# S5 lag matrices formed from the turned sources in one stage, M put together by copies within SBUF, and S5 stages and selection rounds at earlier units of the attention loop

## The reference, cut to what matters

```python
# S5 mixer: 32 groups of 16 channels, 64 complex states each, 512 steps
bu = einsum('blgc,gpc->blgp', u, bb)                   # complex, bb = coef * b
x  = associative_scan(x[l] = lb * x[l-1] + bu[l])      # lb = exp(a * dt)
y  = real(einsum('blgp,gcp->blgc', x, c)) + d_skip * u
y  = gelu(y);  y_ssm = y * sigmoid(y @ w_glu + b_glu)

# sparse attention: 8 heads of 64; an indexer picks 128 keys for each query
s_idx  = sum_h relu(qi[h] @ ki.T) * wi[h]              # causal
sel    = top_k(s_idx, 128)
y_attn = softmax(q @ k[sel].T * scale) @ v[sel]
```

## Time and profile before

| | us |
|---|---|
| median of 3 runs | 750.1 (749.08 to 751.55) |
| the profiled execution | 751.51 |
| its span, first to last instruction | 749.7 |
| PE busy | 703.4 (94%) |
| DVE busy | 478.8 (64%) |
| ACT busy | 310.5 (41%) |
| POOL busy | 258.4 (34%) |

### The profile page before, as it was taken

How to read it: one execution, slowest core, us unless ns; L and a number is a source line. 1 busy time by engine, 2 the same in 40 slices (tenths; PEclk the granted TensorE clock), 3 DMA queues, 4 the chain that set the end, 5 groups by cost and what they waited for, 6 DMA issues and landing times.

```text
span 749.7 us, 9853 instructions
## 1 busy us (share of the span) xinstructions
PE 703.4 (94%) x3566; PEld 555.2 (74%) x3566; DVE 478.8 (64%) x818; ACT 310.5 (41%) x487; POOL 258.4 (34%) x211
## 2 busy tenths in 40 slices
PE   0899999999878999999999999999999999999997
PEld 0687777777555656778798888888878887888886
DVE  2868987976999789788757867655654555000005
ACT  4435346745612564723475344344334344122120
POOL 2001899419902400000003443443342442443440
PEclk9899999999987989999899999999999999999999
DMA  9942131260065665826733223323323313313302
GB/s 335 379 127 85 57 112 57 85 196 1 8 71 51 185 237 190 296 76 225 259 106 113 84 84 112 105 63 112 100 68 113 97 71 113 103 66 112 113 1 112
DMA packets 63081, 91.47 MB, mean 122 GB/s; under 512 B 12010, under 2 KB 41474, under 8 KB 62979
## 3 DMA queue, kind: packets, MB, share of 16 engines
q1 hardware_dynamic: 59520, 89.44, 37.8%
q10 hardware_dynamic: 3523, 1.54, 0.7%
HBM read 86.28 MB, written 4.69 MB: 121 GB/s over the span
## 4 chain that ended last, share of the span: by engine, by line
PE 76%; DVE 15%; ACT 3%; issue 2%; DMA 2%; SPq 0%; ACTq 0%; DVEq 0%
PE bank L1615 22%; PE bank L1617 22%; PE bank L1616 22%; PE bank L1620 3%; DVE arena L1318 2%; PE bank L1965 1%; PE bank L1850 1%; DVE stat L1315 1%; DVE w_lo L1167 1%; DVE arena L1157 1%; DVE arena L1181 1%; PE bank L1830 1%; PE bank L1960 1%; DMA stat<-in_k_norm 1%; DMA xh<-in_x 1%
## 5 line engine op out<-in xcount | busy, mean ns | idle before, releaser
L503 POOL TENSOR_TENSOR w_lo<-w_raw,w_hi 128x2048 fp32r<-128x2048 f32 x32 | 147.7, 4616 | 349.1 <-ACT w_hi L1048 280.2
L1615 PE MATMUL bank<-act_hi,w_hi 128*128 128x512 f32 (+1 forms) x384 | 145.3, 378 | 0.1
L1617 PE MATMUL bank<-act_hi,w_lo 128*128 128x512 f32 (+1 forms) x384 | 144.3, 376 | 0.0
L1616 PE MATMUL bank<-act_lo,w_hi 128*128 128x512 f32 (+1 forms) x384 | 144.3, 376 | 0.0
L1615 PE MATMUL bank<-w_hi,act_hi 128*128 128x512 f32 x240 | 101.4, 423 | 1.4 <-DVE act_lo L1207 1.4
L1617 PE MATMUL bank<-w_hi,act_lo 128*128 128x512 f32 x240 | 97.4, 406 | 0.0
L1616 PE MATMUL bank<-w_lo,act_hi 128*128 128x512 f32 x240 | 97.4, 406 | 0.0
L700 ACT ACTIVATE w_hi<-w_raw 128x2048 fp32r<-128x2048 f32 x26 | 49.8, 1914 | 93.9 <-PE bank L1617 90.8
L1615 PEld LDWEIGHTS bank<-act_hi,w_hi 128*128 128x128 f32 x384 | 72.3, 188 | 14.6 <-DVE conv L1571 0.3
L1616 PEld LDWEIGHTS bank<-act_lo,w_hi 128*128 128x128 f32 x384 | 72.4, 188 | 14.3 <-issue 0.2
L1617 PEld LDWEIGHTS bank<-act_hi,w_lo 128*128 128x128 f32 x384 | 72.3, 188 | 14.1
(11 more groups left out here) (314 smaller groups left out, 1143.1 us busy)
## 6 DMA issues: line engine op xcount, KB each, us to landing
w_raw<-in_w_up SPq DMA_DIRECT2D x44, 512.0 KB, 4.7
arena<-in_w_ada SPq DMA_DIRECT2D x18, 1024.0 KB, 8.5
w_raw<-in_w_down SPq DMA_DIRECT2D x22, 512.0 KB, 3.9
w_raw<-in_w_in SPq DMA_DIRECT2D x10, 1024.0 KB, 5.1
xh<-in_x SPq DMA_DIRECT2D x8, 512.0 KB, 7.1
w_raw<-in_w_out SPq DMA_DIRECT2D x4, 1024.0 KB, 10.2
arena<-in_w_ada SPq DMA_DIRECT2D x2, 2048.0 KB, 10.9
arena<-lag_dram SPq DMA_DIRECT2D x16, 128.0 KB, 5.9
```

The source lines that it names most:

```text
L503: nc.gpsimd.tensor_tensor(w_lo[:, slot, 0:width], w_raw[:, slot, 0:width], w_hi[:, slot, 0:width].bitcast(F32), ALU.subtract).then_inc(S[" ...
L1615: T.matmul(dst, lhs_hi, rhs_hi, start=start, stop=False)
L1616: T.matmul(dst, lhs_hi, rhs_lo, start=False, stop=False)
L1617: return T.matmul(dst, lhs_lo, rhs_hi, start=False, stop=stop)
```

## The change

The lag matrices are formed in one stage for both halves, at unit 6. The stationary operand is `s5_vt` (the sources as they were before their transposition, 64 rows by 128 columns: 8 powers times 16 channels), the moving operand is `s5_c`, 16 columns. D is added by a matmul with rows of the identity, so `bb_diag`, `add_d` and the lag-0 part of `lag_w` go, and with them `lag_dram`. The result stands on 128 partitions (8 lags times 16 channels), and M is made by 8 copies for each half within SBUF, each shifted down by 16 partitions; POOL clears what no copy writes, after the stage, since M lies where `s5_vt` was. `u` of half 1 gets memory of its own. `y` now also waits for `lag_w` itself. Stages move: lags 7 and 10 to 6, u 6 and 12 to 7 and 8, states 11 and 13 to 9 and 11; y stays at 14 and 15. Three selection rounds run before the loop, and the others are spread differently. ACT's casts move from units 3 and 5 to 9 and 13.

```diff
-         6: ("u", 0, 0), 7: ("lags", 0, 0), 10: ("lags", 1, 0), 11: ("states", 0, 0), 12: ("u", 1, 0), 13: ("states", 1, 0),
+         6: ("lags", 0, 0), 7: ("u", 0, 0), 8: ("u", 1, 0), 9: ("states", 0, 0), 11: ("states", 1, 0),
          14: ("y", 0, 0), 15: ("y", 1, 0), 18: ("g", 0, 0), 20: ("g", 1, 0),
-ROUNDS = {**{i: 2 for i in range(8)}, **{i: 4 for i in range(8, 12)}, 16: 3, 17: 3, 18: 2, 19: 1, 20: 2, 21: 2, 22: 2, 23: 1}
+AHEAD = (1, 1, 1)
+ROUNDS = {**{i: (1, 1) for i in (0, 1, 2, 4, 5)}, 3: (1, 1, 2, 2, 2), 6: (1, 2), 7: (2, 2),
+          8: (2, 2, 2), 9: (2, 2), 10: (2, 2, 2), 11: (2, 2),
+          **{i: (3, 3) for i in range(13, 18)}, **{i: (3,) for i in range(18, 24)}}
...
-        s5_m = [cut(a, NG, P) for a in (26024, 28072)]
-        s5_u = [v.rearrange("p (g n) -> p g n", g=NG) for v in (s5_mem[:, 4096:5120], up32[:].rearrange("p a n -> p (a n)"))]
+        s5_m = [cut(a, CHUNK, NG, CH) for a in (26024, 28072)]
+        s5_u = [v.rearrange("p (g n) -> p g n", g=NG) for v in (s5_mem[:, 4096:5120], cut(23976, 1024))]
-        lags = [cut(a, GH, CHUNK, CH)[0:2 * CH] for a in (26024, 28072)]
+        lags = cut(22440, 2, GH, 2, CH)
...
@@ sync @@
-            sp.wait_ge(S["zeros_stored"], 32)
+            sp.wait_ge(S["lags_ready"], 2)
+            sp.wait_ge(S["m_zero"], 2)
             for half in range(2):
-                sp.wait_ge(S["lag_d_added"], 2 * half + 2)
-                gs = slice(NG * half, NG * (half + 1))
-                for q in range(2):
-                    sp.dma_start(lag_dram[:, gs].rearrange("c (g q) l h -> c q g l h", q=2)[:, q, :, CHUNK - 1:, :],
-                                 lags[half][CH * q:CH * q + CH]).then_inc(S["lags_stored"], 16)
-                sp.wait_ge(S["lags_stored"], 32 * (half + 1))
-                for j in range(CHUNK):
-                    load(s5_m[half][CH * j:CH * (j + 1)].rearrange("p g (l h) -> p g l h", l=CHUNK),
-                         lag_dram[:, gs, CHUNK - 1 - j:2 * CHUNK - 1 - j, :], "m_loaded")
+                for i in range(CHUNK):
+                    n = CH * (i + 1)
+                    load(s5_m[half][0:n, i], lags[P - n:P, half].rearrange("p g q h -> p (g q) h"), f"m_loaded{half}")
...
@@ gpsimd @@
-            nc.gpsimd.memset(s5_mem[:, 0:2048], 0.0).then_inc(S["zero_ready"], 1)
-            nc.gpsimd.memset(bb_diag, 0.0).then_inc(S["bb_zero"], 1)
...
-                G.tensor_copy(w[:, 0, :, 0, :], s5_c[:, 0, gs])
-                G.tensor_copy(w[:, 1, :, 0, :], s5_c[:, 1, gs])
...
-                for q in range(2):
-                    hp = slice(64 * q, 64 * q + 64)
-                    link(G.tensor_copy(bb_diag[hp, :, :, CH * q:CH * q + CH], s5_bb[hp]))
...
             weigh_lags(0)
+            pool.wait_ge(S["lag_mm"], 1)
+            for half in range(2):
+                G.memset(s5_m[half][:, 0:CHUNK - 1].rearrange("p i g h -> p (i g h)"), 0.0).then_inc(S["m_zero"], 1)
             weigh_lags(1)
...
@@ scalar @@
-            for i in range(2):
-                act.dma_start(lag_dram[:, NG * i:NG * (i + 1), 0:CHUNK - 1, :],
-                              s5_mem[0:CH, 0:NG * (CHUNK - 1) * CH].rearrange("p (g l h) -> p g l h", g=NG, l=CHUNK - 1)
-                              ).then_inc(S["zeros_stored"], 16)
...
                     elif stage == "lags":
-                        act.wait_ge(S["lag_mm"], 2 * half + i + 1)
-                        nc.scalar.activation(lags[half][:, 4 * i:4 * i + 4],
-                                             src[0:2 * CH, :].rearrange("p (g l h) -> p g l h", g=4, l=CHUNK),
+                        act.wait_ge(S["lag_mm"], 1)
+                        nc.scalar.activation(lags[:, :, :, i, :], src[:, 0:256].rearrange("p (b g h) -> p b g h", b=2, g=GH),
                                              ACT.Copy).then_inc(S["lags_ready"], 1)
...
-                if i == 3:
+                if i == 9:
                     hi(U_GLU)
-                if i == 5:
+                if i == 13:
                     hi(U_OUT)
...
@@ vector @@
+            top_k([(t,) for t in AHEAD], ())
...
-                        if stage == "lags" and back == 1:
-                            add_d(half)
...
@@ tensor @@
                 elif stage == "u":
                     pe.wait_ge(S["u_grouped"], 2)
-                    pe.wait_ge(S["v_ready"], 8)
-                    if half:
-                        pe.wait_ge(S["state_read"], 1)
+                    pe.wait_ge(*((S["lags_ready"], 2), (S["u_t_read"], 2))[half])
...
                 elif stage == "lags":
+                    pe.wait_ge(S["bb_ready"], 1)
+                    pe.wait_ge(S["v_ready"], 8)
+                    rows = slice(P - 2 * CH, P)
+                    for q in range(2):
+                        T.matmul(bank[6 + q][:, 0:256].rearrange("p (b g h) -> p b g h", b=2, g=GH), ident[rows, :],
+                                 d_eye[:, :, :, q, :], start=True, stop=False)
+                    for g in range(GP):
+                        for r in range(2):
+                            for q in range(2):
+                                hp = slice(64 * q, 64 * q + 64)
+                                ins = T.matmul(bank[6 + q][:, CH * g:CH * g + CH],
+                                               s5_vt[g // GH][hp, r, g % GH].rearrange("p j h -> p (j h)"),
+                                               s5_c[hp, r, g, :], start=False, stop=(g == GP - 1 and r == 1))
+                    ins.then_inc(S["lag_mm"], 1)
...
                 else:
-                    pe.wait_ge(S["lags_ready"], 2 * half + 2)
-                    pe.wait_ge(S["m_loaded"], 16 * CHUNK * (half + 1))
+                    pe.wait_ge(S["lag_w_ready"], half + 1)
+                    pe.wait_ge(S[f"m_loaded{half}"], 16 * CHUNK)
...
-                            T.matmul(o[NCH * q:NCH * (q + 1)], s5_u[half][:, 2 * g + q, :], s5_m[half][:, 2 * g + q, :],
-                                     start=True, stop=False)
+                            T.matmul(o[NCH * q:NCH * (q + 1)].rearrange("c (i h) -> c i h", i=CHUNK),
+                                     s5_u[half][:, 2 * g + q, :], s5_m[half][:, :, 2 * g + q, :], start=True, stop=False)
```

More of the change, by code:

```diff
@@ L175, in layer @@
         ki_w = cut(19616, TT, TAIL)
-        d_eye = cut(25000, GP, CH)[0:2 * CH]
+        d_eye = cut(25000, 2, GH, 2, CH)[P - 2 * CH:P]
         b_glu_row = cut(25512, 512)[0:1]
@@ L192, in layer @@
         prob, prob_t = cut(14336, 2, 512), cut(15360, 2, 512)
-        lag_w = [cut(16384, 2, GH, CHUNK + 1, CH), cut(12032, 2, GH, CHUNK + 1, CH)]
+        lag_w = [cut(a, 2, GH, CHUNK, CH) for a in (16384, 12032)]
         turn = cut(8192, 2, GP, NCH)
@@ L576, in s5_rest @@
                 cf_r, cf_i, ur, ui, r8, w1, w2, w3, w4 = (s5_p[:, i] for i in (12, 13, 17, 18, 19, 20, 21, 22, 23))
-                mag, sin_t, cos_t, mask = s5_p[:, 1], s5_p[:, 8], s5_p[:, 9], s5_p[0:2 * CH, 2]
+                mag, sin_t, cos_t = s5_p[:, 1], s5_p[:, 8], s5_p[:, 9]
                 def square(o_r, o_i, a_r, a_i):
@@ L651, in _ @@
                 turn_step(n)
-            s5_diagonals()
+            skip_diagonals()
             future(1)
@@ L747, in _ @@
                     load(b_glu_row, ssm_b_glu, "b_rows_loaded")
-                    for q in range(2):
-                        load(d_eye[CH * q:CH * q + CH],
-                             ssm_d[0].rearrange("(g q h) -> q g h", q=2, h=CH)[q].partition_broadcast(CH), "d_loaded")
+                    load(d_eye.rearrange("p b g q h -> p (b g q h)"), ssm_d[0].partition_broadcast(2 * CH), "d_loaded")
                 if k % 4 == 0:
@@ L909, in s5 @@
                         act.wait_ge(S["u_t"], 2 * half + i + 1)
-                        if half and i == 0:
-                            act.wait_ge(S["lag_w_ready"], 2)
                         nc.scalar.activation(s5_u[half][:, 8 * i:8 * i + 8], src[:].rearrange("p (g n) -> p g n", g=8),
@@ L1208, in split @@
                        ready)
-            dve.wait_ge(S["zeros_stored"], 32)
             lr, li, ldt = (vec_cols[:, a:a + GP] for a in (C_ARE, C_AIM, C_LDT))
@@ L1385, in heads_out @@
                                        rinv[:, w].unsqueeze(2).broadcast_to([P, HEADS, HD]), ALU.mult), "y_attn_ready")
-            def add_d(half):
-                for i in range(2):
-                    dve.wait_ge(S["lags_ready"], 2 * half + i + 1)
-                    g = 4 * i
-                    signal(V.tensor_tensor(lags[half][:, g:g + 4, 0, :], lags[half][:, g:g + 4, 0, :],
-                                           d_eye[:, GH * half + g:GH * half + g + 4, :], ALU.add), "lag_d_added")
             def scan(half, part):
@@ L1466, in _ @@
                         stage, half, part = S5_AT.get(j - back, ("none", 0, 0))
-                        if stage == "lags" and back == 1:
-                            add_d(half)
-                        elif stage == "states" and back == 1:
+                        if stage == "states" and back == 1:
```

(27 more changed lines are left out.)

28 lines of the change are left out of this document (11 added, 17 removed).

## The result

The changed kernel takes **761.5 us** (median of 4, 761.04 to 762.59) where the kernel before, run beside it, takes 749.6 (748.09 to 751.55): ratio 1.0207, 95% interval 1.0158 to 1.0255. Ratios are estimated from the fast runs of both kernels, so they need not be the quotient of the two medians shown. The forecast was 758, in a range of 747 to 766. The sign came, and the time lies inside the range, but above the forecast's own 756 to 760: the loss of 11.9 us falls in the band of rival 3 (+10 to +18), which had a chance of 0.12. Nor did it come the way I had worked out: the first matmul of `y` half 0, Y0, is 14.5 us late where I had 7.8, and 4.9 of it came back later, where I had nothing coming back. Profiled: span 759.3 (us 761.51), granted clock 0.966; before 749.7, 0.970.

A forecast was written before the change was run, and what follows sets the result against it. DVE was taken to pace the loop up to the first y matmul and PE after it. That matmul comes 7.8 us later and nothing comes back: 750.1 + 7.8 = 758, range 747 to 766.

The forecast's parts named there:

- rival 3: Lag stage: loads queue or PE runs at 1.2 GHz, stage 14.6 to 17 us, total 764 to 767; chance 0.12.
- What bounds the loop: Loop of 32 attention units: DVE paces the part up to the first y matmul, PE the part after it.
- Up to the lag stage: Units 4 to 9: unit 8's logits at 194.1, DVE ready at 201.2, lag stage begun at 192.2.
- AHEAD: Before the loop: three selection rounds, 2.95 us, move into DVE's gap before the first logits, free.
- The lag stage: PE at unit 6: 128 records at 60 ns plus D, 8.6 us, bounds 5.1 and 14.6 at full clock.
- The lock: scan(0): DVE operations with two SBUF inputs take turns with POOL's weigh_lags, costing 3.6 us, bounds 0 and 8.
- Units 12 and 13: DVE: logits 0.8, all of scan(1) 10.6 and two rounds at 512 keys 3.04, together 14.4 us.
- the signs that I had named: Trace checks, among them PE idle over 20 us between 205 and 243; wrong if lag stage outside 5 to 15.
- After Y0: Rest of the loop behind the first y matmul: order unchanged, PE without idle time, so nothing of the 7.8 us comes back.
- rival 2: After the first y matmul DVE paces, so 9.1 us of removed rounds come back, total 747; chance 0.18.
- SP's copies: SP queue: 16 copies within SBUF, 0.47 us each to issue, issued by 211.6, hidden by 26 us.
- M read with a step of 256: y matmuls: 16 pieces of 16 columns per matmul, cost taken as 0, between 0 and 2 us.

The follow-up runs named there:

- e1: Changed kernel with the imaginary half of the lag matmuls left out, 64 records instead of 128: 754.2 us, ratio 1.0136.
- e6: Changed kernel with the lag stage cut in two halves of 64 records, scans later, weigh_lags(1) ahead, unit 13's rounds given to 14 and 15: 755.6 us, ratio 1.0138.
- e9: Changed kernel with 64 moving columns instead of 16 per lag record, written to columns nobody reads, lag products left out: 758.07 us in a single profiled run.
- e12: e11 with lag records of 64 and 48 moving columns instead of 16 and the skip term as wide, output still correct: 750.2 us, ratio 1.0036.
- e2: Changed kernel with five 128x512 identity matmuls put between the narrow ones of the lag stage: 769.8 us, ratio 1.0305.
- e3: Changed kernel with the states of half 1 back at unit 13, so scan(1) runs behind unit 14's logits: 755.1 us, ratio 1.011.
- e4: Changed kernel with weigh_lags(1) on POOL before its wait for the lag stage: 758.4 us, ratio 1.0169.
- e7: Changed kernel with both scans back at their old places (states at 11 and 13), single lag stage kept: 753.9 us, ratio 1.0122.
- e11: e6 with e8's order of rounds, none between unit 12's logits and scan(1): 753.5 us, ratio 1.0112.
- e10: The kernel before, unedited, profiled once more on e8's chip: 749.45 us.
- e5: Kernel before with only the change's earlier selection (AHEAD) and new distribution of rounds: 747.1 us, ratio 1.0032.
- e8: e5 with the four rounds of units 13 and 14 moved to 15 to 17, so none stand ahead of scan(1): 746.1 us, ratio 1.0041.

## Why the prediction came near, and where it was wrong

**What bounds the loop.** Right: the loss is decided at Y0, DVE paces up to it, PE behind it.

**Up to the lag stage.** Right within 0.8 us, which is the later start of the loop (169.52 against 168.75). AHEAD and unit 3's rounds were free; unit 8's logits 194.68 (forecast 194.1), DVE ready at 201.7 (201.2), the stage begun at 192.87 (192.2).

**The lag stage: the step that failed.** I had 8.6 us and measured 13.63, and the path from its end to logits 10, at the lower level too, 6.4 for 4.2. With the 0.7 of the later start, logits 10 came at 212.9 instead of 205.0: +7.9. The 13.63 lies inside the 5 to 15 us outside which I had called myself wrong: those bounds were drawn at full clock and could not see this. The price of a record was right, 56 to 59 ns against 60, in e1, e6, e9 and e12; what was mis-sized is the level at which it is paid. Rival 3 had the lower level (stage 14.6 to 17), with a chance of 0.12, and I took it from the old stage, where PE had been idle ahead. Here PE was not. In the seven kernels with 16-column records in full number (the changed one, e2, e3, e4, e6, e7, e11), the clock fell within 4.1 us of the first record; in the two with 48 or 64 columns, one profile each, it did not fall in the stage; e1's 64 records were followed by a fall as e6's were. That it depends on what the records stream is shown by the pair e9 and after, and again by e12 and e11; why it does so was not measured. The five wide matmuls of e2 did not help; whether more of them would is open.
The Trainium skill, "TensorE: Matmul & The Clock Gate", section "HAM oscillation — how this bites in real kernels", puts the fall down to stretches in which TensorE sits idle. In this case's trace PE is busy 13.63 of 13.63 us and the clock falls at 195.5; the measurement decides: a busy share of 100% in the profile is no guarantee. By the same page's section "LDWEIGHTS (loading the stationary operand)", which I had weighed, the 128 loads would take 13.7 us at full clock, an estimate from its figure. e9 measured 7.36 us for 128 records, each load 188 ns long and the next one begun after 57: loads overlap more than that rule has it. That they do so because they alternate between the row halves is my reading; no run leaves the alternation out. That the page's figure lies at the measured 13.6 is coincidence.

**The lock.** Too dear: 1.65 us instead of 3.6, inside its bounds, because POOL had shifted with the stage and only one operation met scan(0). In e9, where the stage was on time, it cost 3.8.

**Units 12 and 13** took 14.5 us (forecast 14.4); unit 14's logits to Y0 2.5 (1.9), at the lower level. The sum: +7.9 - 1.9 + 0.1 + 0.6 = 6.7, from 243.5 to 250.2. Of the signs that I had named, one more failed by a little: from the stage's end to Y0 PE idled 19.1 us, not over 20.

**After Y0.** "Nothing comes back" was wrong by 4.9 us. 3.7 of them lie in the loop, beyond the 3 that I had named as a refutation, but not for rival 2's reason (DVE pacing there). The stretches from Y0 to unit 31's logits, of before, of before again (e10) and of after:

```profile
235.74:306.19 70.45, 67.32 (x438) 43.87 (x438) 61.73 (x119) 36.82 (x81) 9.03 (x2) 0.90 0.53 182
```
```profile
235.17:302.97 67.80, 64.40 (x431) 41.86 (x432) 61.56 (x117) 36.02 (x79) 9.02 (x2) 0.95 0.54 185
```
```profile
250.19:316.91 66.72, 62.28 (x439) 41.08 (x438) 49.36 (x96) 36.76 (x81) 3.65 (x1) 0.98 0.55 194
```

DVE has 12 us less to do in the last than in the first two (49.36), and that bought nothing visible: the same program needs 2.65 us less when its clock is 0.95 and not 0.90, and the changed one continues that line at 0.98. The other runs agree: e2, with DVE as little busy as in the changed kernel (49.4 us) but the clock at 0.93, takes 68.2 us, and e3, with DVE at 57.5 and the clock at 0.95, 67.2. Of the 4.9 us, 3.7 came back here and the rest behind the loop, where before has one low stretch of 6.8 us and after one of 3.4. So PE paces, as I had it, and the level decides how fast. That the median came within 3.5 us of 758 is partly luck: this gift, which I had not foreseen, and the cheaper lock stood against the dearer stage.

**SP's copies** took 0.63 us each to issue, not 0.47; issued by 219.9 for a Y0 at 250, hidden as forecast. M read with a step of 256 showed no cost. A piece is 16 columns and a matmul reads 8 of them, not the 16 of the prediction; the four records of a group with M take 0.44 us at full clock before (242.41) and in e3 alike, and 0.69 at the lower level before and after (Y0's own row):

```profile
242.41 0.44 PE L1960 MATMUL bank<-arena,s_mem 128*64 128x128 f32 x4
```
```profile
246.61 0.44 PE L1930 MATMUL bank<-arena,s_mem 128*64 128x128 f32 x4
```

**What stays open.** Timed, e5, e8 and e12 stand at 1.003 to 1.004. From unit 4's to unit 31's logits e8 takes 118.9 us and e12 117.3, but e10, the kernel before, 117.4: at its better clock it has nothing left to win here. Timed runs of before lie between 739 us at 0.99 and 757 at 0.97, those of e12 between 744 at 0.98 and 761 at 0.96; where the low stretches lie in the timed runs no trace shows.

## What to carry to other kernels

Price a stage of many small matmuls at both levels of TensorE's clock, and look at the granted clock in the trace rather than at its busy share: here a record's price doubled in the middle of the stage (56 to 107 ns) with the engine 100% busy. Where records are paid by their loads, streaming more columns into unused PSUM may cost nothing: here 128 records took 7.4 us with 64 columns each, and the clock stayed full in the stage, though not behind it. Before moving work of the pacing engine ahead of a consumer, list every gate of that consumer: Y0 had three (unit 14's logits, the bank that scan(1) frees, PE's own queue), and taking one away only showed the next.

## What the runs showed of the hardware that I had not expected

- 64 fp32 records of 64x128 stationary and 16 moving columns, alternating between the row halves, take 3.75 us, and 128 of 64 columns 7.36 (e9), 64 of 48 columns 3.77 (e12): 57 to 59 ns a record at full clock for 16, 48 and 64 columns.
- The granted clock fell to 0.5 in or right behind the first block of 16-column records in all eight kernels that have one, with PE without a gap, and in e11 again in the second; e6's second block ran at 0.5 from its start. Once it stayed there for 34 us (e2), in spite of wide matmuls at five places in the block.
- A copy within SBUF takes 0.63 us to issue on SP's queue (16 in 10.15), a load from DRAM 0.47.
- DVE's `tensor_tensor` with both inputs in SBUF took 2.24 to 2.84 us beside one of POOL's and 0.69 alone (L1384, L1385); those that read PSUM (L1380 to L1383) took 0.68 beside POOL.
- One program, two profiles: 749.7 and 747.7 us of span, with the first y matmul 67.0 and 63.1 us behind the first logits, by where the low stretches fall.
